# A hybrid diffusion backbone: five of ten modulation vectors summed by VectorE ahead of TensorE

## The reference, cut to what matters

```python
s_lat = jax.nn.silu(c)
s_ctx = jax.nn.silu(c_ctx)
for l in range(DEPTH):
    sh1, sc1, g1, sh2, sc2, g2 = jnp.split((s_lat @ w_mod[l] + b_mod[l])[:, None, :], N_MOD, axis=-1)
    mod_c = s_ctx @ w_mod[l] + b_mod[l]
    ...
    h = h + g1 * token_mix(xn @ w_in[l], k_c, v_c, lp, cos, sin)
    h = h + g2 * sq_relu_mlp(rmsnorm(h, norm2_g[l]) * (1 + sc2) + sh2, w_ff1[l], w_ff2[l])
```

## Time and profile before

| | |
|---|---|
| runs | 1393.94, 1395.88, 1396.25 us |
| median | 1395.88 us |
| span of the profiled execution | 1393.0 us |
| PE busy | 1354.4 us, 97% |
| weight loads of PE | 1110.7 us, 80% |
| DVE busy | 779.3 us, 56% |
| ACT busy | 549.3 us, 39% |
| POOL busy | 192.9 us, 14% |
| granted TensorE clock, mean | 0.992 |
| moved by DMA | 205.28 MB, 147 GB/s on the mean |

### The profile page before, as it was taken

How to read it: one execution, slowest core, us unless ns; L and a number is a source line. 1 busy time by engine, 2 the same in 40 slices (tenths; PEclk the granted TensorE clock), 3 DMA queues, 4 the chain that set the end, 5 groups by cost and what they waited for, 6 DMA issues and landing times.

```text
span 1393.0 us, 19645 instructions
## 1 busy us (share of the span) xinstructions
PE 1354.4 (97%) x8084; PEld 1110.7 (80%) x8084; DVE 779.3 (56%) x1127; ACT 549.3 (39%) x849; POOL 192.9 (14%) x179
## 2 busy tenths in 40 slices
PE   8989999999999999999999999999999999999997
PEld 3558756777787887777778888888769999899996
DVE  5544675244448666644223443367866788765663
ACT  6652373232223332433112331144555444553552
POOL 1251000612200042000000002200004404100012
PEclk9999999999999999999999999999999999999998
DMA  9333302544541363244453226424325647455551
GB/s 377 126 110 106 121 2 106 174 151 152 196 151 46 108 250 141 91 151 160 147 177 106 91 94 224 150 82 138 108 74 180 225 135 273 152 187 191 182 195 63
DMA packets 55289, 205.28 MB, mean 147 GB/s; under 512 B 6261, under 2 KB 6645, under 8 KB 53664
## 3 DMA queue, kind: packets, MB, share of 16 engines
q1 hardware_dynamic: 52992, 194.22, 40.4%
q0 software_dynamic: 2208, 9.81, 2.0%
HBM read 200.86 MB, written 3.15 MB: 146 GB/s over the span
## 4 chain that ended last, share of the span: by engine, by line
PE 90%; DVE 3%; ACT 2%; POOL 1%; DMA 1%; issue 1%; SPq 0%; DVEq 0%; ACTq 0%; POOLq 0%
PE ps L1547 27%; PE ps L1549 26%; PE ps L1548 26%; PE ps L1848 2%; PE ps L1576 2%; PE ps L1859 1%; PE ps L1874 1%; DMA pairs<-in_pairs 1%; PE ps L1946 1%; PE ps L1958 1%; PE ps L1804 1%; DVE k_t L1270 1%; DVE wl L1034 1%; PE ps L1601 1%; POOL envelope L637 0%
## 5 line engine op out<-in xcount | busy, mean ns | idle before, releaser
L1547 PE MATMUL ps<-xh,wh 128*128 128x512 f32 (+2 forms) x1392 | 473.1, 340 | 2.6 <-DVE xl L1101 1.4
L1034 DVE TENSOR_TENSOR wl<-raw,wh 128x1024 fp32r<-128x1024 f32 (+2 forms) x272 | 352.3, 1298 | 218.1 <-ACT wh L723 215.1
L1548 PE MATMUL ps<-xl,wh 128*128 128x512 f32 (+2 forms) x1392 | 466.1, 335 | 0.0
L1549 PE MATMUL ps<-xh,wl 128*128 128x512 f32 (+2 forms) x1392 | 465.8, 335 | 0.0
L723 ACT ACTIVATE wh<-raw 128x1024 fp32r<-128x1024 f32 (+2 forms) x272 | 283.5, 1043 | 320.6 <-PE ps L1549 320.2
L1547 PEld LDWEIGHTS ps<-xh,wh 128*128 128x128 f32 (+1 forms) x1392 | 260.3, 187 | 44.9 <-issue 14.5
L1548 PEld LDWEIGHTS ps<-xl,wh 128*128 128x128 f32 (+1 forms) x1392 | 261.8, 188 | 27.7 <-issue 1.0
L1549 PEld LDWEIGHTS ps<-xh,wl 128*128 128x128 f32 (+1 forms) x1392 | 260.2, 187 | 29.2
L1547 PE MATMUL ps<-hid_h,wh 128*128 128x512 f32 (+1 forms) x512 | 172.5, 337 | 0.0
L1548 PE MATMUL ps<-hid_l,wh 128*128 128x512 f32 (+1 forms) x512 | 171.7, 335 | 0.0
L1549 PE MATMUL ps<-hid_h,wl 128*128 128x512 f32 (+1 forms) x512 | 171.6, 335 | 0.0
(11 more groups left out here) (252 smaller groups left out, 1444.4 us busy)
## 6 DMA issues: line engine op xcount, KB each, us to landing
raw<-in_units SPq DMA_DIRECT2D x262, 512.0 KB, 3.3
mod_ring<-in_mod_units SPq DMA_DIRECT2D x49, 512.0 KB, 4.0
gap_hy<-in_mod_units SPq DMA_DIRECT2D x15, 512.0 KB, 5.5
pairs<-in_pairs SPq DMA_DIRECT2D x6, 1024.0 KB, 14.3
gap_relu<-in_mod_units SPq DMA_DIRECT2D x7, 512.0 KB, 4.6
raw<-in_units SPq DMA_DIRECT2D x6, 384.0 KB, 2.9
h<-in_x SPq DMA_DIRECT2D x4, 512.0 KB, 7.3
mod_ring<-in_pairs SPq DMA_DIRECT2D x2, 1024.0 KB, 15.1
```

The costliest lines, as they stand in the source:

```text
L1034: dve.tensor_tensor(wl[:, g % SLOTS, 0:n], raw[:, g % SLOTS, 0:n], wh[:, g % SLOTS, 0:n].bitcast(F), ALU.subtract)\
L1547: pe.matmul(dst, w_h, m_h, start=first, stop=False)
L1548: pe.matmul(dst, w_h, m_l, start=False, stop=False)
L1549: return pe.matmul(dst, w_l, m_h, start=False, stop=last)
```

## The change

For vectors 2, 3, 4, 7 and 8 (`SUMMED`) the product over units is taken from PE. Behind a main unit VectorE does `weigh(i)`: it multiplies the unit's 128x1024 weights by the activation of each partition (a pointer to one column of `silu_wide`) and adds it up in SBUF over the eight units, once per stream: tensor_scalar for a vector's first unit, scalar_tensor_tensor for the seven others; two streams for vectors 2, 3, 4 and 7, one for vector 8. Then PE does `mod_sum(v)`: it sums over partitions with a column of ones (`picks`), four matmuls per stream, of the same shape as in `mod_unit`. The ring's buffer is free for the next load when VectorE has weighed the unit. The patterns change too: single units behind most mains instead of pairs behind every second or third, starting in gate_c1, and "s" marks the sum, which goes behind the main unit that came last before it in the pattern. By the plan the last weighing and the sum stand so: vector 2, unit 23 and the sum both behind the second unit of pool; vector 3, unit 31 and the sum both behind the second of gate_a1; vector 4, unit 39 behind the third of pool_out and the sum behind the first of hy; vector 7, unit 63 and the sum both behind the 15th of ff1a; vector 8, unit 71 and the sum both behind the eighth of ff2a. Pool's third and fourth main and each of gate_a2's three are followed by two units. Room for the sums comes from the norms' tiles (`norm_room`) and from `gained`; `roped` and `conv_v` move elsewhere.

```diff
@@ -63,19 +63,19 @@
         def with_mods(pattern):
-            return pattern if first else pattern.replace("m", "").replace("t", "")
+            return pattern if first else pattern.replace("m", "").replace("t", "").replace("s", "")
         out += [(layer, *p) for p in [
...
             ("gate_c0", "MMMM"),
-            ("uq", "MMM"), ("ukv", "MM"), ("gate_c1", "MMMM"),
-            ("wo", with_mods("MMmmMMmm")),
-            ("pool", with_mods("MMmmMMmm")),
-            ("gate_a0", with_mods("MMmm")), ("gate_a1", with_mods("MMmmM")), ("pool_w", "M"),
-            ("gate_a2", with_mods("MMmmMmm")), ("pool_out", "MMMM"),
-            ("hy", with_mods("MMmmMMmmMMmmMMmmMMMM")), ("gate_b0", "MMM"), ("gate_b1", "MMM"), ("gate_b2", "MM"),
+            ("uq", "MMM"), ("ukv", "MM"), ("gate_c1", with_mods("MmMmMmMm")),
+            ("wo", with_mods("MmMMmM")),
+            ("pool", with_mods("MmMmsMmmMmm")),
+            ("gate_a0", with_mods("MmMm")), ("gate_a1", with_mods("MmMmsMm")), ("pool_w", "M"),
+            ("gate_a2", with_mods("MmmMmmMmm")), ("pool_out", with_mods("MMMmM")),
+            ("hy", with_mods("MsMMMMMMMMMMM")), ("gate_b0", "MMM"), ("gate_b1", "MMM"), ("gate_b2", "MM"),
             ("hy_out", "MMMM"),
             ("w_out", "MMMMMMMM" + (16 if first else 8) * "t"),
-            ("ff1a", with_mods("MMMMMMMMmmMMMmmMMMmmMMmm")), ("ff2a", with_mods("MMmmMMMmmMMMmmMMMmmMMmmMMMm")),
+            ("ff1a", with_mods("MMMMMMMMmMmMmMmMmMmMmMmsM")), ("ff2a", with_mods("MmMmMmMmMmMmMmMmsMMMMMmmMMMm")),
             ("ff1b", 16 * "M"), ("ff2b", 16 * "M" + with_mods(13 * "t")),
@@ -100,6 +100,9 @@
         self.tail = []
+
+
+SUMMED = (2, 3, 4, 7, 8)
 
@@ -122,6 +125,15 @@
                     p.after[j].append(("copy", turn))
+            elif kind == "s":
+                p.after[j].append(("sum", mod // KB - 1))
+                p.after[j].append(("copy", mod // KB - 1))
+                order.append(("sum", mod // KB - 1))
+                turn, lead = mod // KB - 1, 0
+            elif mod // KB in SUMMED:
+                p.after[j].append(("weigh", mod))
+                order.append(("unit", mod))
+                mod += 1
             else:
@@ -152,6 +164,8 @@
     for kind, i in order:
+        if kind == "sum":
+            continue
         if kind == "main":
@@ -162,7 +176,7 @@
                 r = RING.index(i)
-                key = at["unit", RING[r - MOD_SLOTS]] if r >= MOD_SLOTS else at["main", 4 * WAVE]
+                key = at["unit", RING[r - MOD_SLOTS]] if r >= MOD_SLOTS else at["main", 3 * WAVE]
         keys.append((key, len(keys), kind, i))
@@ -177,6 +191,23 @@
 RING = [i for kind, i in ORDER if kind == "unit" and i not in GAP_SLOTS]
+
+
+def streams_of(v):
+
+    return 2 if v < VECTORS + 2 else 1
+
+
+def weighed_before(i):
+
+    v, k = divmod(i, KB)
+    return sum(KB * streams_of(u) for u in SUMMED if u < v) + streams_of(v) * k
+
+
+DONE = {}
+for _kind, _i in ORDER:
+    if _kind == "sum" or _kind == "unit" and _i // KB not in SUMMED:
+        DONE[_kind, _i] = len(DONE) + 1
 UNIT_WIDTHS = {PHASES[layer, name].g0 + j: n for layer in range(DEPTH) for name, n in (("kpe", KB * ROPE), ("uq", 2 * QL), ("pool_w", 512))
@@ -232,9 +263,10 @@
         wl = alloc(ctx, "wl", (SLOTS, 1024), R)
-        sq_sum = alloc(ctx, "sq_sum", (T,))
-        sq = alloc(ctx, "sq", (2, T))
-        rstd = alloc(ctx, "rstd", (T,))
+        norm_room = alloc(ctx, "norm_room", (4 * T,))
+        sq_sum, rstd = norm_room[:, 0:T], norm_room[:, 3 * T:4 * T]
+        sq = norm_room[:, T:3 * T].rearrange("p (a t) -> p a t", t=T)
+        picks = alloc(ctx, "picks", (36,))
         params = alloc(ctx, "params", (PARAMS,))
@@ -327,7 +359,7 @@
             probs_t = [probs_t01[:, 0, :, :], probs_t01[:, 1, :, :], probs_t2]
-            roped = sq[:, :, :].rearrange("p a (b t) -> p a b t", t=SEQ)
+            roped = probs_t2[:, :, :].rearrange("p (a b) t -> p a b t", b=2)
         with ExitStack() as s:
@@ -350,7 +382,7 @@
             halves = alloc(s, "halves", (4, HY))
-            conv_v = sq[:, 0, :]
+            conv_v = x0[:, HYB - 1, :]
 
@@ -375,6 +407,9 @@
                      "ff2b": [gap_xl[:, a, :] for a in range(4)] + [gap_relu[:, a, :] for a in range(7)]}
+
+        weighted_of = {v: norm_room[:, :].rearrange("p (s c) -> p s c", c=D) for v in (2, 3, 4)}
+        weighted_of |= {v: gained[:, :, :].rearrange("p a b -> p (a b)").rearrange("p (s c) -> p s c", c=D) for v in (7, 8)}
 
@@ -411,6 +446,7 @@
         mod_done = sem("mod_unit_multiplied")
+        picks_clear, picks_ready, weighed = sem("picks_clear"), sem("picks_ready"), sem("weights_times_silu")
         mod_copied = sem("mod_rows_copied")
@@ -559,7 +595,11 @@
                     elif RING.index(i) >= MOD_SLOTS:
-                        sp.wait_ge(mod_done, RING[RING.index(i) - MOD_SLOTS] - MOD_FIRST + 1)
+                        before = RING[RING.index(i) - MOD_SLOTS]
+                        if before // KB in SUMMED:
+                            sp.wait_ge(weighed, weighed_before(before) + streams_of(before // KB))
+                        else:
+                            sp.wait_ge(mod_done, DONE["unit", before])
                     else:
@@ -728,7 +768,7 @@
             def copy_mod(v):
-                act.wait_ge(mod_done, KB * (v + 1) - MOD_FIRST)
+                act.wait_ge(mod_done, DONE["sum", v] if v in SUMMED else DONE["unit", KB * v + KB - 1])
                 if v > MOD_FIRST // KB:
@@ -962,6 +1002,8 @@
                         act.wait_ge(zv_ready[layer], i)
+                    elif third == 2 and i == HYB - 1:
+                        act.wait_ge(zv_ready[layer], HYB)
                     if third == 0 and i == 0:
@@ -1038,6 +1080,27 @@
                         add_mod(v)
+                    elif what == "weigh":
+                        weigh(v)
+
+            def weigh(i):
+
+                v, k = divmod(i, KB)
+                before = weighed_before(i)
+                if k == 0:
+                    if v == SUMMED[0]:
+                        dve.wait_ge(silu_ready, 1)
+                    else:
+                        dve.wait_ge(mod_done, DONE["unit", KB * v - 1] if v - 1 not in SUMMED else DONE["sum", v - 1])
+                weight, loaded, value = mod_slot(i)
+                dve.wait_ge(loaded, value)
+                for st in range(streams_of(v)):
+                    acc, by = weighted_of[v][:, st, :], silu_wide[:, k, st:st + 1]
+                    if k == 0:
+                        dve.tensor_scalar(acc, weight, by, None, ALU.mult).then_inc(weighed, 1)
+                    else:
+                        dve.wait_ge(weighed, before - streams_of(v) + st + 1)
+                        dve.scalar_tensor_tensor(acc, weight, by, acc, ALU.mult, ALU.add).then_inc(weighed, 1)
 
@@ -1107,7 +1170,7 @@
                     if v == 2 and part == 0:
-                        dve.wait_ge(mod_done, GAP_XL_LAST - MOD_FIRST + 1)
+                        dve.wait_ge(mod_done, DONE["unit", GAP_XL_LAST])
                     product(part, 0)
@@ -1173,10 +1236,13 @@
             dve.memset(silu_wide[:, :, :], 0.0).then_inc(silu_clear, 1)
-            dve.memset(sq_sum[:, :], 0.0).then_inc(idle_clear, 1)
+            dve.memset(sq_sum, 0.0).then_inc(idle_clear, 1)
+            dve.memset(picks[:, :], 0.0).then_inc(picks_clear, 1)
             dve.wait_ge(silu_sig, 1)
...
             dve.tensor_tensor(silu_wide[:, :, 0:2], silu[:, :, :], param("c", KB, 2), ALU.mult).then_inc(silu_ready, 1)
+            dve.wait_ge(picks_clear, 1)
+            dve.memset(picks[:, 1:2], 1.0).then_inc(picks_ready, 1)
             def pair_squares(c):
@@ -1577,6 +1643,19 @@
 
+            def mod_sum(v):
+
+                if v >= 4:
+                    vectors_ready(pe, v - 1)
+                elif v == 2:
+                    pe.wait_ge(picks_ready, 1)
+                pe.wait_ge(weighed, weighed_before(KB * v) + KB * streams_of(v))
+                for st in range(streams_of(v)):
+                    for j in range(4):
+                        mm = pe.matmul(ps[32 * j:32 * j + 32, mod_bank(v), 0:MOD_COLS], picks[:, 1 - st:33 - st],
+                                       weighted_of[v][:, st, j * MOD_COLS:(j + 1) * MOD_COLS], start=st == 0, stop=st == streams_of(v) - 1)
+                mm.then_inc(mod_done, 1)
+
             def turn_mod(v):
@@ -1590,6 +1669,8 @@
                         mod_unit(i)
+                    elif what == "sum":
+                        mod_sum(i)
 
@@ -1666,7 +1747,7 @@
                 for _ in range(count):
-                    pe.matmul(ps[:, 0, :], sq_sum[:, 0:128], sq_sum[:, :], start=True, stop=True)
+                    pe.matmul(ps[:, 0, :], sq_sum[:, 0:128], sq_sum, start=True, stop=True)
 
...
             warm(5)
```

## The result

The changed kernel takes 1414.59 us (median of 4 runs, 1412.78 to 1417.77) where the kernel before takes 1394.91 on the same chip (1393.28 to 1396.25). The ratio is 1.0141, with an interval of 1.0127 to 1.0156: 19.7 us slower. The forecast was 1412, in a range of 1390 to 1422. Its direction and size held, but the terms for waits and clock were together 6 us too high, and a term of some 8 us was missing.

The account below looks back on a forecast made before the run. PE was taken to bound the kernel (busy 97%). Gain -19.3, waits +26.7 and clock +9.0 made +16.4 on 1395.9, so 1412.3 us, with a range of 1390 to 1422.

Parts of the forecast that it names:

- The page first, a microsecond of PE's queue is a microsecond: PE's queue: time taken off counts fully; 20 pairs (25.0 us) less sums (5.75) gain 19.3 if PE never waits.
- Price of a weighing, 1.29, or 1.25 back to back: VectorE: a scalar_tensor_tensor of 1024 columns takes 1.29 us, 1.25 when two follow each other; tensor_scalar about 0.75.
- The rival of half rate, 1.06 more: VectorE: scalar_tensor_tensor of two float32 SBUF tensors takes 1.06 us more on each of 63; +46, 1458; chance 0.04.
- Waits by program order: PE waits at sums whose last weighing follows the same main: vector 7 4.75, vector 8 2.4, vector 2 at least 2.7.
- Alternation with GpSimd: Pool stretch: VectorE and GpSimd take turns, a VectorE instruction costing 1.1 plus GpSimd's 1.1 to 1.3; vector 2 waits 4.6.
- Vector 3, 10.4: PE's wait at vector 3's sum: VectorE needs 38 us with GpSimd taking turns, against PE's 27.6, so 10.4.
- 13 us taking turns, and only some 3 of it in VectorE's pauses: Vector 3: GpSimd's 11 window-mean instructions of groups 3 and 4 delay VectorE, except some 3 us within its pauses.
- Small waits: PE waits 2.9 in pool_out, 0.2 in wo, 0.4 in pool_w and 1.0 at hy's first bank.
- The clock, 3 x 3 = 9.0: Behind the waits of vectors 2, 3 and 7 PE's clock falls, each fall costing about 3 us; 9.0 together.
- The new places ... picks and the memsets cost nothing.: SBUF and program start: new places of roped and conv_v, picks and the memsets add no time.
- layer 1 should keep its time: After ff2a of the first layer none of the effects appear, so layer 1 takes as long as before.
- the rivals: Collisions but clock holds or falls once, 1405 (0.20); little collision, 1394 (0.16); no fall either, 1391 or less (0.20).

Follow-up runs that it names:

- sums_later: The changed kernel with the sums of vectors 2, 3, 7 and 8 one main unit later: 1392.51 us, ratio 0.9988 to the kernel before.
- no_window_means: The changed kernel with GpSimd's window sums left out of layer 0, so its output is not the reference's: 1402.16 us, ratio 1.0058.
- fillers: The changed kernel with unread matmuls on PE ahead of the sums of vectors 2, 3 and 7: 1409.94 us, ratio 1.0108.
- after_aligned: The changed kernel with picks 64 floats long instead of 36, so later tiles start at 0 modulo 64 bytes: 1408.1 us, ratio 1.0089.

## Why the prediction was right, and where not

- *The page first, a microsecond of PE's queue is a microsecond.* Right: 18.5 of 19.3 come back when nothing waits at a sum.
- *Price of a weighing, 1.29, or 1.25 back to back.* Right: 1.28 and 1.24; tensor_scalar 0.75 as forecast. The rival of half rate, 1.06 more, is refuted by the group of L1103, median 1280 ns at 1024 columns. (The Trainium skill, Vector Engine (DVE) Microarchitecture Reference, section Points that are easy to get wrong, says that such an instruction with two sources that aren't bf16 has half the throughput, but not of what. Half of a split's it is not, for that is a tensor_tensor with two sources and takes 1.23; tensor_scalar, with one source, takes 0.75, so against that the trace doesn't contradict it. The prediction's "the trace disagrees" holds for the first reading alone.)
- *Waits by program order.* Right: 4.75, 2.4 and, with collision, 4.6 were forecast for vectors 7, 8 and 2; 4.7, 2.4 and 4.5 were measured, and sums_later takes them away.
- *Alternation with GpSimd.* Right in kind and taken from a single tensor_tensor row: no_window_means shows it. (By the Trainium skill, SBUF — State Buffer, section Who interferes with whom, an instruction with two SBUF inputs and a GpSimd one that reads SBUF contend; this trace agrees, 2.1 against 1.24 for scalar_tensor_tensor.)
- *Vector 3, 10.4.* The mis-sized term: 8.5. "Alone that holds PE up 0.5" was right (0.45 in no_window_means). The step that failed is "13 us taking turns, and only some 3 of it in VectorE's pauses": the collision costs 8.5 - 0.45 = 8.0, where I had 9.9.
- *Small waits.* pool_out 2.6 for 2.9 and hy 0.6 for 1.0; I found none of those of wo and pool_w. All waits together: 23.3 for 26.7.
- *The clock, 3 x 3 = 9.0.* The mechanism was right: the three waits named are followed by falls, and PE kept busy has none. The size was too high: by the windows it is 1.7, 2.0 and 2.6, and fillers gives 4.6 for the three together. The mis-sized term is the price of one fall, which I took from two falls near the start as about 3, and which was 2.1 in the mean. For the waits of 2.4 and 2.9 I added nothing, "with up to 6 more as the upper bound"; in the first profile that held, and in the other four, four of eight such waits brought 1.7.
- *"The new places ... picks and the memsets cost nothing."* Wrong, and the largest miss: picks costs 7 to 9 us. I asked what picks does and not what its length does to the tiles behind it. For the same reason "layer 1 should keep its time" is wrong.

The total, -19.3 + 23.3 + 6.3 + 8 = +18.3 against 19.7 measured, leaves 1.4 and lies inside the ratio's interval (17.7 to 21.8 us); the fall in layer 1, 1.7, would fill the gap. The forecast of +16.4 was close because two errors of opposite sign, +6 and -8, met in it, and that is luck. What decided between slower and no change was vector 3's collision and the falls of the clock, as the rivals had it; but without picks' length the change would have cost 10 by the terms at their measured sizes, or 12 by after_aligned: still slower.

## What to carry to other kernels

A sum or a signal that hangs on an engine's last instruction belongs one unit of the waiting engine later than the code's symmetry suggests; here that alone, with nothing else edited, was worth 21 us (1.0141 to 0.9988). Before work is moved to an engine that is idle, look which other engine works on SBUF in that stretch (GpSimd made a weighing of 1.24 us one of 2.1), and move only what lies elsewhere. And when a tile is added, write down the addresses of the operands behind it: compare the mean of an untouched matmul group in both kernels before anything else is explained.

## What the runs showed of the hardware

- A 128x512 float32r product whose moving operand starts 32 bytes past a multiple of 64 follows the last by 0.234 us instead of 0.2267 at full clock (3%); means of 396 to 399 against 389 to 393 ns. At 256 columns the groups differ by 0.7% (72.4 against 71.9 us). At 64 bytes past a multiple of 128 it is 0.2288 us for 512 columns and 72.5 us for the group of 256; the whole kernel took 1.0013 (1.0001 to 1.0025) of the time.
- scalar_tensor_tensor on two float32 tensors in SBUF: 1280 ns for 1024 columns, 1.24 us each back to back, 2.1 us each while GpSimd works on SBUF too; tensor_scalar 750 ns. GpSimd's own instruction is slowed from 1.09 to 2.1 at the same time, so both sides pay.
- Idle times of PE of 3.7 us or more at a sum, twelve in six profiles, were each followed by a stretch below the full clock; in the first profile those of 4.33, 8.32 and 4.57 us cost 1.7, 2.0 and 2.6 us, so the longest was not the dearest. Of ten between 2.2 and 2.7 us four were followed by one, 1.7 us each, and two executions of the same kernel differ in it. Filling the wait with matmuls nobody needs kept the clock at 1.00.
